# Forgetting attention: two heads by turns, and their scores by three products each on 64-row tiles of the array

## The reference, cut to what matters

```python
log_f = log_sigmoid(f_logit + f_bias)
cum = cumsum(log_f, axis=1)
s = einsum('bqhd,bkhd->bhqk', q, k) * HEAD_DIM ** -0.5
s = s + cum_q[..., None] - cum_k[:, :, None, :]
s = where(k_pos <= q_pos, s, -1e30)
p = softmax(s, axis=-1)
o = einsum('bhqk,bkhd->bqhd', p, v)
```

## Time and profile before

| | |
|---|---|
| median of three runs | 2346.28 us |
| the profiled execution, its own time | 2350.45 us |
| its span, first to last instruction | 2347.6 us |
| granted TensorE clock, mean | 0.99 |
| PE busy | 2267.5 us, 97% of the span |
| DVE, ACT, POOL busy | 54%, 38%, 25% |
| forgetting attention, first score product to end of the last value product | 1309.18 to 1558.58 us: 249.4 us |

### The profile page before, as it was taken

One profiled execution on the slowest core, in us unless ns is written; L12 is line 12 of the kernel. 1 busy time (PEld: TensorE's weight loads), 2 busy tenths in 40 slices (PEclk: granted clock), 3 DMA queues, 4 the chain that ended last, 5 costly groups with the idle time before them and its releaser, 6 DMA issues.

```text
span 2347.6 us, 33170 instructions
## 1 busy us (share of the span) xinstructions
PE 2267.5 (97%) x11544; PEld 1838.3 (78%) x11544; DVE 1263.6 (54%) x1981; ACT 892.9 (38%) x1622; POOL 575.7 (25%) x424
## 2 busy tenths in 40 slices
PE   7998898999999999999999999999899999999998
PEld 6876686888888788878888777778688888878887
DVE  5659568444444434346332688866855444443422
ACT  3027434333333312322221688854433333331223
POOL 2423332223322000110000466642232222200011
PEclk9999999999999999999999999999899999999999
DMA  6340441222221723223443766654122222262312
GB/s 224 101 106 2 153 153 44 91 80 80 80 80 63 251 75 113 90 77 130 150 147 97 181 158 161 161 162 148 45 81 80 82 89 89 71 219 81 130 46 80
DMA packets 268727, 261.16 MB, mean 111 GB/s; under 512 B 32480, under 2 KB 237536, under 8 KB 263664
## 3 DMA queue, kind: packets, MB, share of 16 engines
q1 hardware_dynamic: 257648, 220.32, 32.0%
q10 hardware_dynamic: 11008, 39.92, 4.4%
HBM read 187.92 MB, written 65.08 MB: 108 GB/s over the span
## 4 chain that ended last, share of the span: by engine, by line
PE 88%; DVE 6%; DMA 2%; SPq 1%; ACT 1%; issue 1%; POOL 1%; DVEq 0%; ACTq 0%; POOLq 0%
PE psum L1726 12%; PE psum L1728 12%; PE psum L1727 12%; PE psum L1996 11%; PE psum L1998 11%; PE psum L2000 11%; PE psum L1901 3%; PE psum L1875 3%; PE psum L1974 2%; PE psum L1975 2%; PE psum L1976 2%; PE psum L1834 1%; PE psum L1835 1%; DMA w_raw<-in_swa_w_in 1%; DVE b_full L1466 1%; DVE set_lo L1485 1%
## 5 line engine op out<-in xcount | busy, mean ns | idle before, releaser
L1996 PE MATMUL psum<-b_hi,a_hi 128*128 128x512 f32 x1232 | 484.5, 393 | 19.4 <-DVE b_lo L1451 19.4
L1998 PE MATMUL psum<-b_lo,a_hi 128*128 128x512 f32 x1232 | 482.7, 392 | 0.0
L2000 PE MATMUL psum<-b_hi,a_lo 128*128 128x512 f32 x1232 | 482.6, 392 | 0.0
L1996 PEld LDWEIGHTS psum<-b_hi,a_hi 128*128 128x128 f32 x1232 | 233.3, 189 | 71.3 <-issue 22.7
L1726 PE MATMUL psum<-set_hi,dw_hi 128*128 128x512 f32 x704 | 274.8, 390 | 3.6 <-DVE set_lo L1485 3.6
L1727 PE MATMUL psum<-set_lo,dw_hi 128*128 128x512 f32 x704 | 273.9, 389 | 0.0
L1728 PE MATMUL psum<-set_hi,dw_lo 128*128 128x512 f32 x704 | 273.9, 389 | 0.0
L2000 PEld LDWEIGHTS psum<-b_hi,a_lo 128*128 128x128 f32 x1232 | 233.3, 189 | 49.0
L1998 PEld LDWEIGHTS psum<-b_lo,a_hi 128*128 128x128 f32 x1232 | 233.3, 189 | 48.7 <-issue 0.5
L737 POOL TENSOR_TENSOR score<-score,inv_l 128x128 f32<-128x128 f32 (+7 forms) x128 | 152.2, 1204 | 366.7 <-DVE inv_l L1319 366.3
L770 POOL TENSOR_TENSOR a_sum<-a_raw 128x512 f32<-128x512 f32 x88 | 115.2, 1309 | 495.4 <-DVE a_lo L1446 434.1
(11 more groups left out here) (208 smaller groups left out, 3770.0 us busy)
## 6 DMA issues: line engine op xcount, KB each, us to landing
a_raw<-in_ffn_w_gate_up SPq DMA_DIRECT2D x88, 512.0 KB, 5.0
hid_scr<-hid_out SPq DMA_DIRECT2D x44, 512.0 KB, 5.7
set_full<-hid_scr SPq DMA_DIRECT2D x22, 1024.0 KB, 6.2
x_t<-x_scr SPq DMA_DIRECT2D x16, 1024.0 KB, 8.0
dw_raw<-in_ffn_w_down SPq DMA_DIRECT2D x32, 512.0 KB, 3.6
x_scr<-x_t ACTq DMA_DIRECT2D x24, 512.0 KB, 2.6
w_raw<-in_fox_w_in SPq DMA_DIRECT2D x22, 512.0 KB, 4.0
w_raw<-in_swa_w_out SPq DMA_DIRECT2D x16, 512.0 KB, 3.9
```

The source lines that it names most:

```text
L1996: T.matmul(out_ps, a_hi[i][:, j, :], b_hi[i][:, j, :], start=not more and j == 0, stop=False, skip_group_check=True)
L1998: T.matmul(out_ps, a_hi[i][:, j, :], b_lo[i][:, j, :], start=False, stop=False, skip_group_check=True)
L2000: last = T.matmul(out_ps, a_lo[i][:, j, :], b_hi[i][:, j, :], start=False, stop=j == KH - 1, skip_group_check=True)
```

## The change

Two heads are now worked on together. The six steps are the same, but each is done for both heads by turns: (s0, head 0), (s0, head 1), (s1, head 0) and so on; a turn of the loop now covers two pairs, since the load buffers alternate from pair to pair. The stacked operands go: head 0 lies in partitions 0 to 63 and head 1 in 64 to 127 of each of q_hi, q_lo, k_hi, k_lo. The scores of a step are three products per head (hi hi, hi lo, lo hi) over 64 rows, issued in pairs, one per head, on the upper and the lower row half of the array; head 0 goes to PSUM banks 0 and 1, head 1 to banks 2 and 3, and so both halves are taken by one step. The value products put head 0 into partitions 0 to 63 and head 1 into 64 to 127, each summed over all blocks of keys: `move`, `join` and the product with `no_keys` go, and `result_high` and `result_low` treat both heads in one instruction of 128 partitions, read from PSUM. `ahead` is 6 for products and scores, 5 for the rest, counted in iterations of one head: 3 steps, and 2 or 3 steps. Loads are per pair: four of 512 KB for the operands, two for the gates, one of 512 KB for the values (before, per head: six of 256 KB, one of 512 KB, one of 256 KB).

```diff
-self.ahead = dict(qk=4, scores=4, exps=3, inverse=3, norm=3) if self.fox else \
+self.ahead = dict(qk=6, scores=6, exps=5, inverse=5, norm=5) if self.fox else \
...
-def fill(self, u, s):
-    return self.unit_fills * u + sum(self.fills[:s])
+def local(self, e, s):
+    return 2 * sum(self.fills[:s]) + e * self.fills[s] if self.fox else self.unit_fills * e + s
...
 def qk(a, u, e, s, b=0):
+    n = a.count(u, e, s)
+    if a.fox and not e:
+        return
     wait(pe, a.max_done if a.fox else a.exp_done, n - (1 if a.fox else 3))
...
-T.matmul(ps, q_hi[:, qs], key[:, cc:cc + ww], start=True, stop=False)
-last = T.matmul(ps, q_lo[:, qs], key[:, cc:cc + ww], start=False, stop=not diagonal)
+for q, k in ((q_hi, k_hi), (q_hi, k_lo), (q_lo, k_hi)):
+    for r in range(2):
+        T.matmul(psum[:, r * SEQ + at1:r * SEQ + at1 + ww], q[rows(r), qs], k[rows(r), cc:cc + ww],
+                 start=q is q_hi and k is k_hi, stop=q is q_lo and not diagonal)
...
-if t == 1:
-    T.matmul(pb[rows(1), 0:P], v[:, 1, :], no_keys[:, :], start=True, stop=True)
 for k in range(t + 1):
     cs = slice(0 if k < t else P, 2 * P)
-    last = T.matmul(pb[rows(k % 2), cs], v[:, k, :], p[:, k, cs], start=k < 2, stop=k >= t - 1)
+    for r in range(2):
+        last = T.matmul(pb[rows(r), cs], v[:, k, rows(r)], fox_p[r][par][:, k, cs],
+                        start=k == 0, stop=k == t)
...
 probs_copy(a, u, e, s)
+if a.fox:
+    if e:
+        score_pair(a, pi, i + a.ahead["scores"] - 1, last, b)
+    if ahead := a_step(a, pi, i + a.ahead["inverse"], last):
+        inverse(a, *ahead)
```

More of the change, by code:

```diff
@@ L52, in trunk @@
         x_t = at("x_t", 0, [P, KD, SEQ])
-        fox_p = [at(f"fox_p{i}", 16 * i, [P, TT, 2 * P]) for i in range(2)]
+        fox_p = [[at(f"fox_p{e}{g}", (6 * e, 12 + 8 * e)[g], [P, (6, TT)[g], 2 * P]) for g in range(2)] for e in range(2)]
         swa_p = [at(f"swa_p{i}", 32 + 2 * i, [P, HALF]) for i in range(2)]
@@ L453, in fox_copied @@
             if f < 0:
[L454 to L457, removed]
+                u, f = u - 1, f + 2 * fox.unit_fills
+            e, s = next((e, s) for s in range(fox.steps) for e in range(2) if f < fox.local(e, s) + fox.fills[s])
+            if f > fox.local(e, s):
+                return fox.p_dve, 2 * (fox.steps - 1) * u + 2 * (s - 1) + e + 1
+            return fox.p_act, 2 * fox.steps * u + 2 * s + e + 1
         def swa_copied(n):
@@ L518, in load_out, with load_heads, load_v @@
                     load_out_w(c0, view, j)
[L520 to L532, removed]
+            def load_heads(a, u, b):
+                wait(sp, a.max_done, 2 * a.steps * (u - 1))
+                q_hi, q_lo, k_hi, k_lo = fox_operands(u, b)
+                for part, q, k in ((0, q_hi, k_hi), (1, q_lo, k_lo)):
+                    sp.dma_start(q[:, :].bitcast(FP32), fox_qk[part][bass.ds(u * P, P), :]).then_inc(a.qk_in[b], 16)
+                    sp.dma_start(k[:, :].bitcast(FP32), fox_qk[part][bass.ds(FOX_H * HD + u * P, P), :])\
+                        .then_inc(a.qk_in[b], 16)
+                for e in range(2):
+                    sp.dma_start(fox_cum(u, e, b)[:, :], cum_scr[bass.ds(2 * u + e, 1), :].to_broadcast([P, SEQ]))\
+                        .then_inc(a.qk_in[b], 16)
+            def load_v(a, u, b):
+                wait(sp, a.pv_done, a.groups * (u - 1))
+                sp.dma_start(fox_v_in[b][:, :, :], fox_v[bass.ds(u * P, P), :, :]).then_inc(a.v_in[b], 16)
             def swap_halves(c):
@@ L926, in probs_high @@
                 blocks = a.blocks[s][0]
-                tb = a.bank_of(u, e, s, 0)[0]
-                act.wait_ge(a.t_done, a.fill(u, s) + 1)
+                tb = a.bank_of(e, s, 0)[0]
+                act.wait_ge(a.t_done, a.fill(u, e, s) + 1)
                 if a.fox:
-                    for dst, src in fox_pieces(blocks, tb, fox_p[par]):
+                    for dst, src in fox_pieces(blocks, tb, fox_p[e][par]):
                         last = nc.scalar.activation(dst, src, ACT.Copy)
@@ L1332, in probs_copy @@
                     wait(dve, a.pv_done, a.groups * u + g - 1)
-                    dve.wait_ge(a.t_done, a.fill(u, s) + 2)
-                    for dst, src in fox_pieces(a.blocks[s][1], a.bank_of(u, e, s, 1)[0], fox_p[g % 2]):
+                    dve.wait_ge(a.t_done, a.fill(u, e, s) + 2)
+                    for dst, src in fox_pieces(a.blocks[s][1], a.bank_of(e, s, 1)[0], fox_p[e][g % 2]):
                         last = V.tensor_copy(dst, src)
@@ L1352, in result_low, with score_pair, pair_dve @@
                         .then_inc(a.o_free, 1)
-            def join(a, u, e, s, pi):
-                g = a.group(s)
-                dve.wait_ge(fox_moved, a.groups * u + g + 1)
-                wait(dve, a.o_free, a.groups * u + g - 1)
-                V.tensor_tensor(joint[g % 2][rows(e), :], bank[O_BANK][rows(0), 0:2 * P], v_low_part[g % 2][rows(0), :],
-                                ALU.add).then_inc(fox_joined, 1)
-            def pair_dve(a, pi, first, last):
+            def score_pair(a, pi, i, last, b):
+                if ahead := a_step(a, pi, i, last):
+                    scores(a, *ahead, (b if i < 2 * a.steps else 1 - b))
+                    scores(a, *a_step(a, pi, i + 1, last), (b if i < 2 * a.steps else 1 - b))
+            def pair_dve(a, pi, first, last, b=0):
                 for i in range(2 * a.steps):
@@ L1885, in pv @@
                     for j in range(a.fills[s]):
-                        pe.wait_ge(*fox_copied(u, sum(a.fills[:s]) + j))
+                        pe.wait_ge(*fox_copied(u, a.local(e, s) + j))
                 else:
-                    pe.wait_ge(*swa_copied(a.count(u, s)))
-                wait(pe, fox_joined if a.fox else a.o_free, a.groups * u + g)
+                    pe.wait_ge(*swa_copied(a.count(u, e, s)))
+                wait(pe, a.o_free, a.groups * u + g)
                 if g == 0 and not a.fox:
```

261 lines of the change are left out of this document (121 added, 140 removed).

## The result

The changed kernel takes 2385.74 us (median of 4 runs, 2384.12 to 2391.83) and the kernel before 2347.02 beside it: a ratio of 1.0167, 95% interval 1.0141 to 1.0193. It is slower by 38.7 us, twice the 19.5 that I had summed. The profiled execution took 2384.12 us (span 2382.3, mean granted clock 0.985), against 2350.45 (span 2347.6, 0.990).

The account below looks back on a forecast made before the run. PE was taken to set the pace at 30.04 us a pair; work of 27.2 plus idle 4.9 made 32.1, 16.5 us more over eight pairs. With 3 for the ends, +19.5 gave 2365 us, 8-in-10 range 2325 to 2388.

Parts of the forecast that it names:

- the copies' place: Head 0's bank-emptying copy stands behind step s + 2's exponential: PE idles 2.0 us after s1 and 2.0 after s5.
- Score products with their changes of tile: PE's row-half score pairs 6.5, masks 1.9 and changes of tile 2.1 us: 10.5 a pair.
- The fourth case: Rival: row halves don't work together, scores 17.0 us, a pair 38.6, whole 2418 us; chance 0.07.
- Value products: PE's 80 value records at 0.09 us plus entering and leaving four runs: 9.4 us a pair.
- Transposes: PE's transposes in the attention stage: 7.3 us a pair.
- Idle: PE's waits: 2.0 us after s1, 2.0 after s5, 0.3 after s3, 0.6 at value runs; 4.9 a pair, bounds 0 and 6.
- The clock: No term in the sum; a clock below 1.00 in the stage was named only as a cause not counted.
- The ends: First scores fill all four banks and the last value run is twice as long: 3 us, between 0 and 6.
- Loads: 3.5 MB a pair instead of 4.5, asked for a whole pair ahead: they stay hidden.
- the likeliest case: Slower, as forecast: 2354 to 2385 us, with scores from 9.0 to 12.1 and idle from 4 to 6; chance 0.50.
- PE's work alone counts: Faster rival: bank always free, a pair takes 27.2 us plus 1.0 or so of waits, whole 2334 us; chance 0.27.

Follow-up runs that it names:

- experiment 4: Changed kernel with both heads' score products read from partitions 0 to 63, so that no two can run together: 2477.25 us, ratio 1.0541.
- experiment 1: Changed kernel with exponentials, inverses and scaling 4 iterations ahead instead of 5, so copies stand ahead of the exponential of s + 2: 2357.5 us, ratio 1.0036.
- experiment 5: Changed kernel with experiment 1's edit, and a pair's last transpose bank being the next in the turn of three: 2345.08 us, ratio 0.998.
- experiment 2: Changed kernel with 18 small useless products put ahead of PE's wait for a transpose bank in s3 and s5: 2371.27 us, ratio 1.0118.
- experiment 3: Changed kernel with three tiles of x_t instead of two loaded ahead of the last value products: 2382.99 us, ratio 1.0137.
- experiment 9: Changed kernel with only a pair's last transpose bank made the next in the turn of three, copies left where they were: 2385.34 us, ratio 1.0155.
- experiment 7: Experiment 5's kernel with two score products over 128 partitions per head instead of three on 64, mixing the heads' keys: 2348.63 us, ratio 0.999.
- 8: Experiment 5's kernel without the mask products, so scores above the diagonal aren't masked: 2335.71 us, ratio 0.9939.

## Why the prediction was wrong

The direction, the mechanism (the copies' place) and its two places held; the size was half of what came. The step that failed is the one from idle time to cost: each wait was costed at its own length, and the clock behind it at nothing. One pair, step by step:

- *Score products with their changes of tile: forecast 10.5, measured 10.5* (9.56 and some 1.0 of entries), partly at the slow clock. 0.23 and 0.11 us to a pair, as bounded from the earlier trace rows. Leaving 512 wide products for a mask takes 0.56 us from the last load (1433.06 to 1433.62), against 0.46 in the earlier trace rows: 0.10 for the change of tile, forecast 0.11. The fourth case is refuted by experiment 4, which also shows that its price was too low: with products that can't run together a pair takes 45.2 to 46.9 us and not 38.6.
- *Value products: forecast 9.4, measured 9.74*, of which some 0.7 is the slow clock; a run is left in 0.17 us and not in the 0.38 of the earlier trace rows, which I had kept. *Transposes: 7.3 and 7.95*, 0.2 of it the slow clock.
- *Idle: forecast 4.9, measured 5.9.* Behind the products of s5 2.27 (forecast 2.0), behind those of s1 2.52 (2.0); the other 1.1 us are short ones (0.9 forecast). Experiments 1 and 5 show that the copies' place is the cause: a pair falls from 34.0 to 28.8 without it.
- *The clock: no term at all.* This is the step that failed. The earlier trace rows had 1.00 for a stage in which PE waited 1.1 us for joint at the longest. I had computed two waits of 2.0 and costed them at their own length alone; that the clock might fall I named only as a cause not counted, and gave no reason for counting it as nothing. Measured: 1.5 us a pair more (experiment 2), 1.6 by the two kinds of pair in experiment 1.
- Together 32.1 was forecast, 34.05 measured: +1.0 of idle, +1.5 of clock, -0.5 of work at full clock. Against 30.04 of before that is 4.0 a pair, 32 us over eight, where I had 16.5.
- *The ends: forecast +3, measured -1.5* (the stage is 30.5 us longer, eight pairs are 32). That error went the other way and hid 4.5 us of the others, which is luck. The first steps of the new order lose less than I thought; I haven't traced why.
- *Loads: "they stay hidden" was right inside the stage and wrong behind it.* I had counted the loads of keys and values and left out x_t, of which the diff moves 1 MB behind the last value product: +4.3 us in the trace, of which some 2 are the load and the rest the clock (experiments 3 and 9).

30.5 + 4.3 make the 34.7 us between the two spans (0.2 is gained ahead of the stage); the medians say 38.7, with an interval of 33 to 45. The band of the likeliest case, 2354 to 2385, was narrower than its own bounds give: scores of 9.0 with idle of 4 make 29.7 a pair and 2347, scores of 12.1 with idle of 6 make 34.8 and 2387. That the result lies near its edge says little for the sum.

Of the rivals, *PE's work alone counts* was wrong for the change as it stands, and nearly right for what it could be: without the waits for copies it is 2345, not 2334, since a wait for a score bank of 15 us takes their place. The row tiles gain little of it, some 2 to 4 us if anything (experiment 7), and 9 are taken by masks with four of the changes of tile (8).

## What to carry to other kernels

Where an order by turns puts "copy out of bank" behind "work on the next operand" on a helper engine, the copy's end is set by the products just made; move the copy ahead of that work before you look at banks, for another bank whose copy stands behind the same instruction gained nothing (experiment 9). Price an idle of PE of some 2 us at more than its length: add what a fall of the clock behind it costs, here 1.5 to 1.6 us, and count one fall a pair as the upper case (seven of eight pairs had one in the changed kernel, three in experiment 1). And of a diff count each load that is moved, also those at the stage's edge that belong to the next one.

## What the hardware showed that I had not expected

- In the changed kernel and in experiments 1 and 9 the clock fell to the 1.2 GHz level inside the stage behind idle times of PE's loads of 2.0 to 2.6 us, mostly for some 3.4 us. Their length doesn't tell the cases apart: in the changed kernel it fell behind 2.52 us and not behind 2.27, in experiment 9 behind 2.27 in seven pairs and behind 2.17 in one, and in experiment 1 behind three of seven waits that all last 2.00. What decides I can't say.
- Two products on different row halves, 64 rows by 128 columns, 512 wide, take 0.23 us together; 128 wide they take 0.11, loads included. On one half two 512 wide take 0.46 to 0.47 (experiment 4).
- Before the change, o_lo takes 1.92 to 2.11 us in 15 of its 64 executions and 0.39 to 0.42 in the others, with both inputs in SBUF in all of them. The 15 begin while POOL is scaling rows 896 wide, and each ends some 0.3 us after POOL does: 1412.51 + 2.05 is 1414.56, and POOL ends at 1414.29.

```profile
1410.52 3.77 POOL L737 TENSOR_TENSOR score<-score,inv_l 128x896 f32<-128x896 f32 x2 [1.74 <-DVE inv_l L1319]
```

With one input in PSUM, as after the change, no o_lo takes more than 0.43 us, at twice the partitions, also where it begins while POOL works. That points to POOL's work as what held it; no run takes that work away.
